# A hybrid two-block model on one core: every second lower part in the query and value sections made by GpSimd

## The chip, the cores and the metric

The kernel runs on one core of a Trainium2 chip. The metric is the device time of one execution in microseconds (us). A core has five engines with a queue of instructions each, and each queue runs in its own order: TensorE (PE; its weight loads are PEld), VectorE (DVE, here "the vector engine"), ScalarE (ACT), GpSimd (POOL) and SyncE (SP, which starts the weight transfers here). Engines wait for each other through semaphores. SBUF is the on-chip memory that all engines read; PSUM holds TensorE's results, in 8 banks of 128x512 f32.

## The reference

The input is 256 tokens of width 1024, in f32. Block one has two layers with two attentions each, block two has two layers of another kind; the change is in block two. Cut to what it touches:

```
h = rmsnorm(x, pre_mix_g);  proj = h @ w_in            # 1024 x D_IN
q, k, v = silu(conv4(concat(dn_q, dn_k, dn_v)))        # causal, 4 taps, each 1024 wide
q, k = l2norm(q) * 128 ** -0.5, l2norm(k)              # 8 heads of 128
o = gated_delta_rule(q, k, v, g, beta)                 # chunks of 64
y_a = (rmsnorm(o) * silu(dn_z)) @ w_up_dn
y_b = window_attention_with_sinks(sw_q, sw_k, sw_v) @ w_up_sw   # 16 query heads of 64
x = x + rmsnorm((sigmoid(gate_a) * y_a + sigmoid(gate_b) * y_b) @ w_o)
x = x + rmsnorm(relu(rmsnorm(x) @ w_ff1) ** 2 @ w_ff2)
```

## The kernel before

**Weights.** Every product with a weight matrix is made from two rounded numbers for each operand: the upper part (`hi`) is the value rounded to the fp32r type, the lower part (`lo`) is the rest. Three matmuls (lines 374 to 376) add hi·xh, lo·xh and hi·xl in PSUM. SP loads weights in units of 512 rows by 512 columns into one of 4 buffers `raw` (`load_unit`). A unit is two pieces: an even and an odd one, each 128 partitions by 1024 columns. ScalarE makes `hi` of a piece (`split_hi`, line 348), the vector engine makes `lo` by a subtraction of two SBUF tensors, `raw - hi` (`split_lo`, line 356). There are 4 buffers of `hi` and of `lo`; TensorE takes 12 matmuls for a piece (`multiply`) and then gives its buffers back. SP reloads a `raw` buffer when both lower parts of its unit are made.

**Order.** The plan (`plan_two`) is a list of steps written out by hand: a step ("piece", g), and after it small steps of other work. Every engine goes through the same list and does its share. At the step of piece g ScalarE makes the upper part of piece g+3 (`LEAD`), the vector engine the lower part of piece g+2 (`LO_LEAD`), and TensorE multiplies piece g.

**The stretch.** A section of 1024 columns is two jobs of 4 pieces. After the sections sq and ba (window attention's queries, keys, values and the gates' inputs) come dk, dq and dv, the inputs of the convolution, that is keys, queries and values. During dq and dv the small steps are:
- window attention, one head a step and three heads in the air: scores on TensorE (lines 1453 and 1454); the masked row maximum on the vector engine (`masked_max`: line 880 with a PSUM and an SBUF input, then 886 and 887 on 128x2 numbers in SBUF); exponentials on ScalarE (1716, 1719); turning on TensorE (1461), ScalarE's copy of the turned (1725), the weighted sum on TensorE (1469 to 1471). The row sums are finished on the vector engine by 1971 (an addition of two 128x2 tensors in SBUF) and 1973, the output by 1978;
- the convolution of the section before: two of four steps turn 2x128 channels (TensorE, line 398), and the vector engine puts the four taps on (1841, and 1843 six times, with one input in PSUM);
- for the keys: squares, their sums on TensorE (1441), copied by the vector engine (1889), and the reciprocal roots on GpSimd (893, 899).

On GpSimd stand, before the stretch, the rotations of the queries (lines 913 to 918), and after it the level masks of the delta rule (2097, 2106).

Of the kernel before, what the change touches and what calls it, by code (L numbers as in the profile page):

```python
# [17 lines left out]
F32 = mybir.dt.float32  # L18
F32R = mybir.dt.float32r
I32 = mybir.dt.int32  # L20
ALU = mybir.AluOpType
# [16 lines left out]
RAW = 4  # L38
RING = 4
LEAD = 3  # L40
LO_LEAD = 2
# [39 lines left out]
class Signals:  # L81
# [4 lines left out]
    def __init__(self, nc, ctx, prefix, tally=None):  # L86
        self.nc, self.ctx, self.prefix, self.tally = nc, ctx, prefix, tally
        self.sems, self.count, self.keys, self.stage = {}, {}, {}, 0

    def sem(self, name):  # L90
        if name not in self.sems:
            self.sems[name] = self.ctx.enter_context(self.nc.semaphore(f"{self.prefix}_{name}"))
        return self.sems[name]
# [167 lines left out]
class Core:  # L261


    def __init__(self, nc, ctx, ins, plans):
        self.nc, self.ctx, self.ins = nc, ctx, ins
        self.pieces = [piece for plan in plans for piece in plan.pieces]
        self.units = [(job, n, plan.layer) for plan in plans for job, n in plan.units]
        sb = lambda name, shape, dt=F32: ctx.enter_context(nc.sbuf_tensor(name, shape, dt))
        sem = lambda name: ctx.enter_context(nc.semaphore(name))
        self.x = sb("x_res", [P, TB, D])  # L270
        self.raw = [sb(f"raw{i}", [P, 4 * CH]) for i in range(RAW)]
        self.hi = [sb(f"hi{i}", [P, 2 * CH], F32R) for i in range(RING)]
        self.lo = [sb(f"lo{i}", [P, 2 * CH], F32R) for i in range(RING)]

        self.xh = [sb(f"xh{i}", [P, KB, S], F32R) for i in range(2)]
        self.xl = [sb(f"xl{i}", [P, KB, S], F32R) for i in range(2)]
        self.buf = [sb(f"buf{i}", [P, TB, D]) for i in range(9)]
        self.scratch = sb("scratch", [P, 5120])
        self.final_row = self.buf[3][:, 0, :]
        self.masks = sb("masks", [P, 3, S])  # L280
        self.square = sb("square", [P, 3 + LEVELS, P])
        self.rope1 = sb("rope1", [P, TB, 4, ROT // 2])
        self.rope2 = sb("rope2", [P, TB, 4, ROT // 2])
        self.ident, self.upper, self.ones = (self.square[:, i, :] for i in range(3))
        self.small = sb("small", [P, 850])
        self.small_used = 0
        self.bank = [ctx.enter_context(nc.psum_tensor(f"bank{i}", [P, CH], F32)) for i in range(8)]
        self.passed = sem("passed")
        self.last_read, self.turn_bank, self.hi_at, self.lo_at = {}, {}, 0, 0
        self.programs = {e: [] for e in ("tensor", "scalar", "vector", "gpsimd", "sync")}  # L290
        self.unit_loaded = [sem(f"unit_loaded{i}") for i in range(RAW)]
        self.hi_ready, self.lo_ready = sem("hi_ready"), sem("lo_ready")
        self.pieces_used = sem("pieces_used")

    def hold(self, s, bank, name, key=0):

        self.last_read[bank] = (s, name, key, s.stage)
# [26 lines left out]
    def load_unit(self, sp, u):  # L324

        job, n, layer = self.units[u]
        if u >= RAW:
            sp.wait_ge(self.lo_ready, 2 * (u - RAW) + 2)
        slot, k = u % RAW, job.unit
        r0 = (job.row + n * k) * P  # L330
        src = self.ins[job.weight][layer, r0:r0 + k * P, job.col:job.col + job.cols].rearrange("(k p) c -> p k c", p=P)
        dst = self.raw[slot][:, 0:k * job.cols].rearrange("p (k c) -> p k c", k=k)
        sp.dma_start(dst, src).then_inc(self.unit_loaded[slot], 16)
# [6 lines left out]
    def split_hi(self, act, upto):  # L340

        for g in range(self.hi_at, min(upto, len(self.pieces))):
# [5 lines left out]
            act.activation(self.hi[g % RING][:, 0:w], src, ACT.Copy).then_inc(self.hi_ready, 1)  # L348
            self.hi_at = g + 1

    def split_lo(self, dve, upto):

        for g in range(self.lo_at, min(upto, len(self.pieces))):
            src, w = self.piece_raw(g)
            dve.wait_ge(self.hi_ready, g + 1)
            dve.tensor_tensor(self.lo[g % RING][:, 0:w], src, self.hi[g % RING][:, 0:w].bitcast(F32),  # L356
                              ALU.subtract).then_inc(self.lo_ready, 1)
            self.lo_at = g + 1

    def multiply(self, pe, g, rows=(0, 1), blocks=(0, 1)):  # L360


        job, n = self.pieces[g]
        pe.wait_ge(self.lo_ready, g + 1)
        k, c, slot = job.unit // 2, job.cols, g % RING
        xh, xl = self.xh[job.xt], self.xl[job.xt]
        for kk in rows[:k]:
            row = job.xt_block + n * k + kk
            w = slice(kk * c, kk * c + c)
            for tb in blocks:  # L370
                out, t = self.bank[job.banks[tb]][:, 0:c], slice(tb * P, tb * P + P)
                first = job.start and n == 0 and kk == 0
                last = job.stop and n == job.pieces - 1 and kk == k - 1
                pe.matmul(out, xh[:, row, t], self.hi[slot][:, w], start=first, stop=False)  # L374
                pe.matmul(out, xh[:, row, t], self.lo[slot][:, w], start=False, stop=False)  # L375
                mm = pe.matmul(out, xl[:, row, t], self.hi[slot][:, w], start=False, stop=last)  # L376
        if rows[-1] >= k - 1 and blocks[-1] == TB - 1:
            mm.then_inc(self.pieces_used, 1)
        return mm
# [79 lines left out]
def rms(pool, s, waits, means, out, key):  # L459

    pool.wait_ge(*s.at("mean", waits[0]))
    pool.tensor_scalar(out, means[0], 1e-6, None, ALU.add).then_inc(*s.up("rms_first", key))  # L462
    pool.wait_ge(*s.at("rms_first", key))
    pool.wait_ge(*s.at("mean", waits[1]))
    pool.tensor_tensor(out, out, means[1], ALU.add).then_inc(*s.up("rms_sum", key))
    pool.wait_ge(*s.at("rms_sum", key))
    pool.tensor_tensor(out, out, s.minus_half[:, 0:out.shape[-1]], ALU.pow).then_inc(*s.up("rms", key))
# [774 lines left out]
def block_two(nc, core, s, plans, ins):  # L1242
# [815 lines left out]
    def _(pool):  # L2058
        for plan in plans:
            layer, base = plan.layer, plan.base  # L2060
            for what in plan.all_steps(s):
                kind, arg = what[0], what[1] if len(what) > 1 else None
                if kind == "rstd":
                    out = t.final_r if s.stage == DEPTH else t1.r[:, s.stage, :]
                    rms(pool, s, [(c, TB - 1) for c in range(2)], [t1.mean[:, s.stage, c, :] for c in range(2)], out, "final" if s.stage == DEPTH else "r")
# [14 lines left out]
                if kind == "post_x":  # L2080
                    tb = what[2]
                    i = 2 * layer + arg
# [117 lines left out]
```

## Time and profile before

| | |
|---|---|
| median of 3 runs | 1938.02 us (1937.54 to 1938.33) |
| the profiled execution | 1939.12 us, its span 1937.3 us |
| granted TensorE clock, mean | 0.987 |
| TensorE busy | 1853.9 us (96%) |
| vector engine busy | 1201.1 us (62%) |
| ScalarE busy | 921.5 us (48%) |
| GpSimd busy | 233.2 us (12%) |

The span is from the first to the last instruction of the profiled execution. Times inside the trace are us from its start; one "x15" is 15 instructions. "[0.42 <-ACT ...]" says that the engine was idle for 0.42 us before this instruction and which engine's instruction ended that. The granted clock is a share of 2.4 GHz. The names in "out<-in" are the program's own; a "buf", "small", "square" or "scratch" lies in SBUF, a "bank" in PSUM. Matmul rows overlap each other, since matmuls are pipelined.

### The profile page before, as it was taken

To read this page: it belongs to the slowest core of one execution; us is meant where nothing else is said; L and a number is where in the kernel's file an instruction comes from. 1 tells how busy PE (TensorE), PEld (TensorE's weight loads), DVE (VectorE), ACT (ScalarE), POOL (GpSimd) and SP (SyncE) were. 2 spreads that over 40 slices of the span, in tenths; PEclk is the share of its full clock that TensorE was granted. 3 is DMA by queue.
4 is the path that set the end of the run, shared out by engine and by line. 5 is a ranking of instruction groups with operands and counts; after the bars stand their busy time and mean duration, and the time that the engine had idled before them with its cause. 6 is when DMAs were issued, how large, how long until landed. Compare 5 with 4: busy or idle time off the path is not lost.

```text
span 1937.3 us, 25474 instructions
## 1 busy us (share of the span) xinstructions
PE 1853.9 (96%) x9623; PEld 1523.1 (79%) x9623; DVE 1201.1 (62%) x2323; ACT 921.5 (48%) x1624; POOL 233.2 (12%) x298
## 2 busy tenths in 40 slices
PE   5999999999999999999999989998999999999998
PEld 4877877887787788778888878887777888877887
DVE  4655667666566766676655665556586555665555
ACT  4354365434436645454433454445464333444443
POOL 0301100030030002102213000000201221200000
PEclk9999999999999999998999999999998999999999
DMA  6543534565343456232212445554433221354552
GB/s 242 165 146 114 169 127 164 168 197 170 109 152 131 139 177 206 99 110 81 72 66 87 153 152 196 174 181 164 135 109 95 66 80 66 113 189 155 174 188 95
DMA packets 136817, 270.15 MB, mean 139 GB/s; under 512 B 5500, under 2 KB 8312, under 8 KB 136696
## 3 DMA queue, kind: packets, MB, share of 16 engines
q1 hardware_dynamic: 134820, 265.75, 41.2%
q10 hardware_dynamic: 1876, 2.78, 0.4%
q8 instruction: 78, 1.28, 0.3%
q14 instruction: 43, 0.35, 0.1%
HBM read 267.46 MB, written 1.05 MB: 139 GB/s over the span
## 4 chain that ended last, share of the span: by engine, by line
PE 82%; DVE 9%; ACT 4%; issue 3%; POOL 1%; DMA 1%; SPq 0%; DVEq 0%; POOLq 0%; ACTq 0%
PE bank L374 21%; PE bank L376 21%; PE bank L375 21%; PE bank L398 3%; PE bank L1522 3%; PE bank L1536 2%; DVE buf L1843 2%; PE bank L1535 1%; DVE lo L356 1%; PE bank L1441 1%; DVE scratch L880 1%; PE bank L553 1%; PE bank L545 1%; ACT scratch L670 1%; PE bank L543 1%
## 5 line engine op out<-in xcount | busy, mean ns | idle before, releaser
L374 PE MATMUL bank<-hi,xh 128*128 128x512 f32 (+1 forms) x2016 | 821.5, 407 | 21.8 <-issue 12.0
L376 PE MATMUL bank<-hi,xl 128*128 128x512 f32 (+1 forms) x2016 | 791.4, 393 | 0.0
L375 PE MATMUL bank<-lo,xh 128*128 128x512 f32 (+1 forms) x2016 | 789.1, 391 | 0.0
L348 ACT ACTIVATE hi<-raw 128x1024 fp32r<-128x1024 f32 (+1 forms) x504 | 527.9, 1049 | 341.0 <-PE bank L376 338.8
L356 DVE TENSOR_TENSOR lo<-raw,hi 128x1024 fp32r<-128x1024 f32 (+1 forms) x504 | 610.7, 1225 | 90.1 <-ACT hi L348 89.7
L374 PEld LDWEIGHTS bank<-hi,xh 128*128 128x128 f32 x2016 | 383.6, 190 | 95.8 <-issue 19.3
L376 PEld LDWEIGHTS bank<-hi,xl 128*128 128x128 f32 x2016 | 382.0, 190 | 83.2
L375 PEld LDWEIGHTS bank<-lo,xh 128*128 128x128 f32 x2016 | 384.2, 191 | 68.9
L1740 ACT ACTIVATE scratch<-bank 128x512 f32<-128x512 f32 x48 | 28.7, 599 | 143.5 <-PE bank L1522 143.5
L398 PE MATMUL bank<-square,buf 128*128 128x128 f32 x584 | 87.9, 273 | 7.2 <-POOL buf L918 5.2
L398 PEld LDWEIGHTS bank<-square,buf 128*128 128x128 f32 x584 | 70.8, 140 | 23.8 <-issue 7.6
L880 DVE CUSTOM_DVE_ANT_0 scratch<-bank,masks 128x128 f32<-128x128 f32 (+1 forms) x128 | 40.6, 355 | 71.5 <-PE bank L545 50.2
L462 POOL TENSOR_SCALAR small<-small 128x1 f32<-128x1 f32 (+1 forms) x13 | 5.1, 390 | 605.1 <-ACT scratch L455 604.9
L1814 DVE TENSOR_TENSOR xl<-bank,xh 128x512 fp32r<-128x512 f32 x32 | 22.1, 692 | 78.1 <-ACT xh L1647 78.1
L1716 ACT ACTIVATE scratch<-scratch,small 128x128 f32<-128x128 f32 x64 | 28.6, 448 | 79.7 <-DVE small L887 79.7
L659 ACT ACTIVATE scratch<-scratch,small 128x128 f32<-128x128 f32 x64 | 28.7, 449 | 75.2 <-DVE small L887 75.2
L1843 DVE SCALAR_TENSOR_TENSOR buf<-bank,small,buf 128x255 f32<-128x255 f32 (+1 forms) x144 | 62.7, 477 | 2.5
L741 DVE TENSOR_SCALAR buf<-bank,small 128x512 f32<-128x512 f32 x48 | 33.8, 746 | 41.2 <-PE bank L376 41.2
L893 POOL TENSOR_SCALAR small<-small 128x4 f32<-128x4 f32 (+1 forms) x14 | 4.5, 324 | 451.3 <-ACT scratch L688 203.8
L2020 DVE TENSOR_TENSOR scratch<-scratch,bank 128x512 f32<-128x512 f32 (+1 forms) x48 | 28.7, 638 | 30.0 <-PE bank L1536 30.0
L1647 ACT ACTIVATE xh<-bank 128x512 fp32r<-128x512 f32 x32 | 19.2, 598 | 59.0 <-PE bank L398 59.0
L880 DVE CUSTOM_DVE_ANT_0 scratch<-bank,masks,small 128x128 f32<-128x128 f32 x64 | 24.1, 413 | 37.0 <-PE bank L1454 37.0
(269 smaller groups left out, 1981.9 us busy)
## 6 DMA issues: line engine op xcount, KB each, us to landing
raw<-in_w_in SPq DMA_DIRECT2D x136, 1024.0 KB, 5.0
raw<-in_w_ff SPq DMA_DIRECT2D x64, 1024.0 KB, 5.2
raw<-in_w_proj_a SPq DMA_DIRECT2D x8, 1024.0 KB, 5.0
raw<-in_w_proj_b SPq DMA_DIRECT2D x8, 1024.0 KB, 5.0
raw<-in_w_out SPq DMA_DIRECT2D x8, 1024.0 KB, 5.1
raw<-in_w_up_sw SPq DMA_DIRECT2D x8, 1024.0 KB, 5.0
raw<-in_w_up_dn SPq DMA_DIRECT2D x8, 1024.0 KB, 5.1
raw<-in_w_o SPq DMA_DIRECT2D x8, 1024.0 KB, 5.6
```

The source lines that it names most:

```text
L348: act.activation(self.hi[g % RING][:, 0:w], src, ACT.Copy).then_inc(self.hi_ready, 1)
L356: dve.tensor_tensor(self.lo[g % RING][:, 0:w], src, self.hi[g % RING][:, 0:w].bitcast(F32), ALU.subtract).then_inc(self.lo_ready, 1)
L374: pe.matmul(out, xh[:, row, t], self.hi[slot][:, w], start=first, stop=False)
L375: pe.matmul(out, xh[:, row, t], self.lo[slot][:, w], start=False, stop=False)
L376: mm = pe.matmul(out, xl[:, row, t], self.hi[slot][:, w], start=False, stop=last)
L398: mm = pe.transpose(bank[:, (j * TB + tb) * P:(j * TB + tb + 1) * P], src[:, tb, c:c + P], core.ident)
L659: ins = act.activation(prob[h % 2][:, 0, cols], masked[:, h % 2, cols], ACT.Exp, scale=SCALE, bias=t.negmax[:, h % 2, tb:tb + 1], accum_ou ...
L741: ins = dve.tensor_scalar(role[name][:, tb, cols], B[job.banks[tb]][:, :], t.r[:, s.stage, tb:tb + 1], None, ALU.mult)
L880: ins = dve.tensor_tensor_reduce(masked[:, cols], bank[:, cols], core.masks[:, which, keys], 1.0, NEG if sink is None else sink[0], ALU.ad ...
L1522: mm = pe.matmul(B[TURN][:, i * P:i * P + P], lm[l % 2][:, h, c, :], tr[g % 2][h][:, c, 0, :], start=True, stop=True)
L1536: mm = pe.matmul(o[:, P:2 * P], yy[:, h, c, :], tr[g % 2][h][:, c, 1, :], start=True, stop=True)
L1843: ins_ = dve.scalar_tensor_tensor(y, x, w, y, ALU.mult, ALU.add)
```

## The change

For the jobs dq0, dq1, dv0 and dv1 of either layer of block two the lower part of the odd pieces is made by GpSimd: 8 of the 16 pieces of a layer. GpSimd issues it at the step two pieces ahead, as the vector engine did, and before the other work of that step. It has its own semaphore, and TensorE and SP wait for the one that belongs to the piece. SP waits for both pieces of the unit one by one. The vector engine passes over these pieces.

```diff
@@ Core.load_unit
-            sp.wait_ge(self.lo_ready, 2 * (u - RAW) + 2)
+            for g in (2 * (u - RAW), 2 * (u - RAW) + 1):
+                sp.wait_ge(*self.lo_done(g))
@@ Core
+    def on_pool(self, g):
+
+        job, n = self.pieces[g]
+        return job.name in ("dq0", "dq1", "dv0", "dv1") and n % 2 == 1
+
+    def lo_done(self, g):
+
+        mine = self.on_pool(g)
+        return self.lo_pool if mine else self.lo_ready, sum(self.on_pool(i) == mine for i in range(g + 1))
+
+    def split_lo_pool(self, pool, g):
+
+        if g < len(self.pieces) and self.on_pool(g):
+            src, w = self.piece_raw(g)
+            pool.wait_ge(self.hi_ready, g + 1)
+            pool.tensor_tensor(self.lo[g % RING][:, 0:w], src, self.hi[g % RING][:, 0:w].bitcast(F32),
+                               ALU.subtract).then_inc(self.lo_pool, 1)
+
     def split_lo(self, dve, upto):
 
         for g in range(self.lo_at, min(upto, len(self.pieces))):
+            self.lo_at = g + 1
+            if self.on_pool(g):
+                continue
             src, w = self.piece_raw(g)
             dve.wait_ge(self.hi_ready, g + 1)
             dve.tensor_tensor(self.lo[g % RING][:, 0:w], src, self.hi[g % RING][:, 0:w].bitcast(F32),
                               ALU.subtract).then_inc(self.lo_ready, 1)
-            self.lo_at = g + 1
@@ Core.multiply
-        pe.wait_ge(self.lo_ready, g + 1)
+        pe.wait_ge(*self.lo_done(g))
@@ block_two, GpSimd's program
                 kind, arg = what[0], what[1] if len(what) > 1 else None
+                if kind == "piece":
+                    core.split_lo_pool(pool, base + arg + LO_LEAD)
```

## Rows read from the trace of the kernel before

**Rows 1.** Page, first part: busy us of each engine (share of the span).

```profile
PE 1853.9 (96%) x9623; PEld 1523.1 (79%) x9623; DVE 1201.1 (62%) x2323; ACT 921.5 (48%) x1624; POOL 233.2 (12%) x298
```

**Rows 2.** Windows: length, busy PE, PEld, DVE, ACT, POOL, granted clock, DMA share, GB/s.

```profile
793.39:876.71 83.32, 81.22 (x434) 63.41 (x434) 64.94 (x211) 45.65 (x116) 3.92 (x2) 0.96 0.28 90
1393.76:1478.77 85.01, 82.91 (x435) 65.54 (x434) 64.92 (x211) 45.64 (x116) 3.93 (x2) 0.94 0.27 88
```

**Rows 3.** Line 1469: its idle time, us and times, by releaser.

```profile
  ACT scratch L1725: 1.6, 4
```

**Rows 4.** Timeline of PE, 1396 to 1413.5: start, us, instruction, idle before.

```profile
1408.24 0.48 PE L374 MATMUL bank<-hi,xh 128*128 128x512 f32 x1
...
1412.52 0.41 PE L1469 MATMUL bank<-buf,scratch 128*128 128x64 f32 x2 [0.42 <-ACT scratch L1725]
```

**Rows 5.** Timeline of ACT, 1396 to 1448.

```profile
1396.14 1.04 ACT L348 ACTIVATE hi<-raw 128x1024 fp32r<-128x1024 f32 x1
...
1406.19 1.04 ACT L348 ACTIVATE hi<-raw 128x1024 fp32r<-128x1024 f32 x1
...
1411.91 0.47 ACT L1725 ACTIVATE scratch<-bank 128x384 f32<-128x384 f32 x1
...
1415.71 1.06 ACT L348 ACTIVATE hi<-raw 128x1024 fp32r<-128x1024 f32 x1
...
1426.09 1.05 ACT L348 ACTIVATE hi<-raw 128x1024 fp32r<-128x1024 f32 x1
...
1447.82 1.04 ACT L348 ACTIVATE hi<-raw 128x1024 fp32r<-128x1024 f32 x1
```

**Rows 6.** Timeline of DVE, 1396 to 1431.

```profile
1398.61 0.23 DVE L886 TENSOR_SCALAR small<-small 128x2 f32<-128x2 f32 x1
...
1398.82 0.15 DVE L1971 TENSOR_TENSOR small<-small 128x2 f32<-128x2 f32 x1
...
1402.58 1.21 DVE L356 TENSOR_TENSOR lo<-raw,hi 128x1024 fp32r<-128x1024 f32 x1
1403.71 0.34 DVE L880 CUSTOM_DVE_ANT_0 scratch<-bank,masks,small 128x128 f32<-128x128 f32 x1
...
1408.67 1.21 DVE L356 TENSOR_TENSOR lo<-raw,hi 128x1024 fp32r<-128x1024 f32 x1
1409.80 0.34 DVE L880 CUSTOM_DVE_ANT_0 scratch<-bank,masks,small 128x128 f32<-128x128 f32 x1
...
1418.72 0.15 DVE L1971 TENSOR_TENSOR small<-small 128x2 f32<-128x2 f32 x1
...
1422.48 1.21 DVE L356 TENSOR_TENSOR lo<-raw,hi 128x1024 fp32r<-128x1024 f32 x1
...
1428.57 1.21 DVE L356 TENSOR_TENSOR lo<-raw,hi 128x1024 fp32r<-128x1024 f32 x1
```

**Rows 7.** Groups by line, DVE, 1393.76 to 1478.77: busy us, mean ns, idle before.

```profile
L356 DVE TENSOR_TENSOR lo<-raw,hi 128x1024 fp32r<-128x1024 f32 x15 | 18.1, 1210 | 0.0
```

**Rows 8.** Lines 2106 and 918: duration in ns, shortest, median, longest; starts; forms.

```profile
L2106 POOL TENSOR_TENSOR scratch<-buf,square x24: 1269/1292/2302, 895.6 to 1625.5; 128x512 f32<-128x512 f32 x24
L918 POOL TENSOR_TENSOR buf<-scratch x24: 323/741/1292, 54.1 to 1380.3; 128x256 f32<-128x256 f32 x20, 128x64 f32<-128x64 f32 x4
```

**Rows 9.** Timeline of POOL, 1395 to 1530, the key norms.

```profile
1467.78 1.00 POOL L893 TENSOR_SCALAR small<-small 128x16 f32<-128x16 f32 x1 [86.75 <-DVE small L1889]
1468.87 2.93 POOL L899 TENSOR_TENSOR small<-small 128x16 f32<-128x16 f32 x1
```

**Rows 10.** Waits of the SP queue, 1380 to 1490: us, times, longest.

```profile
SPq L333 <- DVE lo L356: 99.7, 9, 16.0
```

**Rows 11.** Timeline of POOL and DVE near 1498; line 2012, durations in ns.

```profile
1497.64 2.25 POOL L2106 TENSOR_TENSOR scratch<-buf,square 128x512 f32<-128x512 f32 x1
...
1498.69 1.74 DVE L2012 TENSOR_TENSOR buf<-square,buf 128x512 f32<-128x512 f32 x1
...
L2012 DVE TENSOR_TENSOR buf<-square,buf x4: 679/1213/1744, 896.6 to 1584.5; 128x512 f32<-128x512 f32 x4
```

More of the change, by code:

```diff
@@ L293, in __init__ @@
         self.pieces_used = sem("pieces_used")
+        self.lo_pool = sem("lo_pool")
     def hold(self, s, bank, name, key=0):
```

## The prediction

> **What bounds the kernel now.** The page's busy row comes first: TensorE is busy for 96% of the span, the vector engine for 62%, GpSimd for 12% [rows 1]. The change touches 16 vector instructions of more than two thousand, so the share says little, and the stretch has to be looked at by itself. In the windows of the query and value sections (from the first product of dq0 to the first of the last piece of dv1, once in each layer) TensorE is busy for 81.22 of 83.32 us and 82.91 of 85.01 us, the vector engine for 64.9 us of either [rows 2]. So TensorE sets the end here too, and what the vector engine is spared counts only where TensorE waits for a chain that runs through it. The list of what TensorE's weighted sums of the window attention (line 1469) waited for names one releaser, the copy of the turned probabilities on ScalarE (line 1725), 4 times in the whole trace and 1.6 us together [rows 3].
>
> The timelines tell what stands behind the longest of these. Of this chain, step by step: scores on TensorE, row maximum on the vector engine (lines 880, 886, 887), exponentials on ScalarE, then ScalarE's copy, then TensorE's sum. At 1412.52 TensorE begins line 1469 after 0.42 us of waiting [rows 4]; the copy began at 1411.91 [rows 5]; it stood behind the exponentials of a maximum begun at 1409.80, and that one behind a lower part from 1408.67, 1.21 us long, itself behind convolution taps and, before these, a maximum at 1403.71 that followed the lower part of 1402.58 [rows 6]. That last one is of an odd piece: it is one that goes.
>
> **The parts of the change.** *Removed from the vector engine:* 8 lower parts in a layer, 16 in all, of 1.21 us each in this stretch [rows 7], 19.4 us of its time. Nearly all of it lies beside TensorE's work. Where it lies on a chain, the gain is bounded by the waits of rows 3: 1.6 us for all four, two in a layer: the one at 1412.52, and one that ScalarE's own work ends. Four steps after the first the same chain recurs and comes out even with TensorE, without a wait that the view lists.
>
> *Added on GpSimd:* 16 subtractions of 128x1024. The trace has none of this size. From both sides: the level masks of 128x512 take 1292 ns (median; 1269 the shortest), the rotation's sum of 128x256 takes 741 [rows 8]. The difference, 551 ns for 256 columns, put on twice gives 1292 + 1102 = 2.39 us. Twice 1292 would be 2.58; the longest GpSimd instruction of 512 columns, 2302 [rows 8], doubled would be 4.6 and is the upper end; the vector engine's own 1.21 is the lower end. I take 2.4, since the two nearest sizes point to it.
>
> *Is it in time?* The upper part is ready by 1397.18 (begun 1396.14, 1.04 long [rows 5]), and TensorE takes up that piece at 1408.24 [rows 4]: 11.1 us for an operation of 2.4. Even 4.6 is covered. GpSimd has nothing else in the stretch but the two instructions of the key norms (1467.78 and 1468.87, 3.93 us busy [rows 2, 9]). The last odd piece stands behind them in GpSimd's order and is then ready near 1474.2, TensorE takes it up at 1478.77, the end of the window of rows 2: 4.6 us left. The first of the two was itself held: 1.00 us, while the lower part of that last piece ran on the vector engine; this goes, and is off the path. If the cover were gone, a piece would be late by what the operation exceeds these 11.1 us by.
>
> *The weight queue:* SP waits for both lower parts before it reloads a buffer, 99.7 us of waiting in 9 times for line 356 in this stretch [rows 10]. It will be released by GpSimd at about 1399.6 in place of 1403.8, and similarly for six more; the last is later by 5.5 us (1474.2 for 1468.7). ScalarE's upper parts don't wait for weights here, so I price both at 0; the added wait instruction of SP costs nothing, as it only stands before transfers that wait anyway. On TensorE one wait is replaced by another.
>
> *The new collision.* An instruction of either engine can be lengthened by the other's. GpSimd's mask at 1497.64 takes 2.25 us against the 1.29 of rows 8, and the vector engine's product of two SBUF tensors (line 2012) at 1498.69 takes 1.74 against 0.68 at the shortest [rows 11]: the later waits until the other's instruction is over. The Trainium skill (SBUF — State Buffer, Who interferes with whom) says that a vector instruction with two SBUF inputs and a GpSimd instruction that reads SBUF exclude each other for the whole instruction; by that rule too, the trace agrees, with 1.06 us on that product. So a GpSimd subtraction of 2.39 us can hold back line 1971 (two small SBUF inputs) and the even lower parts of line 356. Taking the second layer, with the ready times of the upper parts from [rows 5] and the vector engine's from [rows 6]:
>
> First case. GpSimd works 1397.2 to 1399.6. Line 1971 wants to begin at 1398.82 and is held to 1399.6: +0.8. The taps behind it end 0.8 later (1403.5), but the lower part of 1402.58 is gone, so the maximum begins at 1403.45 in place of 1403.71 (−0.26). The next upper part (1406.19) moves with it to 1405.93, and GpSimd works 1407.0 to 1409.4. The vector engine is through with its taps at 1408.67 − 0.26 = 1408.4, wants the even lower part and is held to 1409.4; the maximum of 1409.80 begins at 1410.55: **+0.75**, and this is on the chain to TensorE's wait at 1412.52.
>
> Second case, everything 0.75 later. Upper part of 1415.71: ready at 1417.5, GpSimd to 1419.9; line 1971 (1418.72 + 0.75 = 1419.47) held by 0.45. The taps end 0.45 later, the lower part that followed them at 1422.5 is gone, so the next maximum comes 0.55 earlier than in step; it moves the upper part of 1426.09 to an end at 1427.3; GpSimd to 1429.75; the even lower part (1428.57 + 0.75 − 0.55 = 1428.8) is held by 1.0; net 1.0 − 0.55 = **+0.45** on a chain that had nothing to spare.
>
> In the value section the GpSimd subtractions fall beside taps, which read one operand from PSUM, and I find no further cost. The sum of a layer is 0.75 + 0.45 = 1.2 us, of both layers 2.4 us. The profiled execution would go from 1939.12 (span 1937.3 and 1.8 around it) to 1941.5. It stands 1.1 us above the median of 1938.02, and the comparison is of medians: 1938.0 + 2.4 = **1940.4 us**.
>
> **The rivals.** *B, the chain gets shorter:* GpSimd's operation is shorter than 2.4 us or falls beside the vector engine's PSUM work; the freed 1.21 us ends the four waits of rows 3, −1.6 us: 1936.4. For it: the even lower part is held only because it comes about 1 us too early in either case, and the freed 1.21 us is more than that. Against it: GpSimd is started by the upper part of the same step in which the even lower part stands, so that the two meet by their order.
>
> *C, the small instructions are held too (slower):* lines 886 and 887 work on one SBUF operand [rows 6], and the maximum can't be told to ScalarE before 887. No row shows one of them beside a GpSimd instruction, so nothing in the trace excludes it. Then it is line 886 at 1398.61 that is held to 1399.6, 0.2 more than in the first case, and 0.4 more in the second; and a third place comes in, the step of the upper part of 1447.82 [rows 5]: GpSimd works from 1448.9 to 1451.3, over the whole of that maximum's small instructions, an estimated 0.4 of it on TensorE. A layer costs 1.2 + 0.6 + 0.4 = 2.2, both 4.4: 1942.4. It decides as soon as the exclusion holds for one-input SBUF instructions. The Trainium skill (SBUF — State Buffer, Who interferes with whom) says that a vector tensor_scalar in a 2-port mode excludes GpSimd as well; no run here shows it yet.
>
> *D, GpSimd's operation is long:* at 3.5 us each of the four holds of a layer grows by 1.1, 4.4 us in a layer: about 1949.
>
> *E, the clock:* the same stretch takes 83.32 us at a granted clock of 0.96 and 85.01 at 0.94 [rows 2], 1.7 us for the same work. If the shift of a few tenths moves a stretch at 1.2 GHz, each layer may change by 1.7 either way: with B, 1936.4 − 3.4 = 1933.0, with A 1943.8.
>
> *F, the vector engine was the bound after all:* −19.4, 1918.6; against it stand the 2.1 us that TensorE is idle in each window.
>
> **How the numbers follow.** A (the forecast) 0.50, B 0.17, C 0.22, D 0.04, E 0.06 (half each way), F 0.01. A measurement of this kernel tells some 0.2% (3.9 us) from no change: faster means below 1934.1, slower above 1941.9. B and most of A lie within. Slower: most of C (0.19), D, half of E and a tail of A (0.04), 0.30. Faster: half of E, F and little more, 0.05. Same: 0.65. The range goes from B less a little to C and a mild D: 1936.0 to 1943.5.
>
> **What would show it.** The GpSimd rows of the new subtraction should have a shortest near 2.4 us; line 1971 a few instances near 0.6 to 1.0 us in place of 0.15; line 356, two or so in a layer of some 2.2 us; TensorE's wait before line 1469 near 1 us where it was 0.42. Line 886 tells A from C: 0.23 in all instances, or some near 1 us. I am wrong if the wait before line 1469 is gone (B), if TensorE waits for GpSimd’s lower part (too late), or if the two windows change by over 3 us with none of these rows.

## The result: 0.28% slower, and what the profile shows after the change

| | before | after |
|---|---|---|
| median of the 14 runs of each kernel | 1937.93 us (1936.03 to 1942.0) | 1943.77 us (1939.85 to 1944.84) |
| ratio to before, 95% interval | | 1.0028 (1.0020 to 1.0037) |
| the profiled execution | 1939.12 us, span 1937.3 | 1942.28 us, span 1940.5 |

The ratio makes 5.4 us (3.9 to 7.2), more than the 0.2% (3.9 us) that a measurement of this kernel was said to tell from no change; only the lower end of the interval touches it. The forecast was +2.4 us, and no measurable change as the likeliest case.

The numbers of lines rise by 22 behind the new code: 356 is now 379, 880 and 886 are 902 and 908, 1469 is 1491, 1725 is 1747, 1971 is 1993, 913 and 918 are 935 and 940. GpSimd's subtraction is line 368. The first row of the page answers to [rows 1]:

```profile
PE 1853.2 (96%) x9623; PEld 1522.8 (78%) x9623; DVE 1193.5 (62%) x2307; ACT 921.6 (47%) x1624; POOL 271.6 (14%) x314
```

16 instructions have gone from the vector engine, but it is busy for only 7.6 us less, where 16 times 1.21 is 19.4 us. Of the other 11.8 us, 5.7 have come back in line 908 and 3.8 in line 379, as held instructions. The last 2.3 us are in the way of counting: the page counts once where two rows overlap, and the durations themselves add up to 9.5 us less (1279.8 before, 1270.3 after). The view by line, duration in ns (shortest, median, longest), shows on which lines; for line 379 the window is the second layer's, 1385 to 1484:

```profile
L368 POOL TENSOR_TENSOR lo<-raw,hi x16: 2359/2382/3400, 790.0 to 1475.8; 128x1024 fp32r<-128x1024 f32 x16
L908 DVE TENSOR_SCALAR small<-small x32: 228/228/1575, 796.6 to 1484.9; 128x2 f32<-128x2 f32 x32
L1993 DVE TENSOR_TENSOR small<-small x32: 143/149/153, 801.4 to 1487.2; 128x2 f32<-128x2 f32 x32
L379 DVE TENSOR_TENSOR lo<-raw,hi x9: 1203/1217/2109, 1388.7 to 1483.0; 128x1024 fp32r<-128x1024 f32 x9
```

Line 908, two numbers per partition with one SBUF input, takes 0.23 us as a rule and up to 1.58. The timelines of GpSimd and of the vector engine (start, us, instruction, idle before), second layer, show why; the vector engine's answer to [rows 6]:

```profile
1402.55 2.38 POOL L368 TENSOR_TENSOR lo<-raw,hi 128x1024 fp32r<-128x1024 f32 x1 [6.63 <-ACT hi L350]
1412.30 2.38 POOL L368 TENSOR_TENSOR lo<-raw,hi 128x1024 fp32r<-128x1024 f32 x1 [7.37 <-ACT hi L350]
...
1454.36 3.40 POOL L368 TENSOR_TENSOR lo<-raw,hi 128x1024 fp32r<-128x1024 f32 x1 [5.68 <-ACT hi L350]
```

```profile
1403.90 1.05 DVE L908 TENSOR_SCALAR small<-small 128x2 f32<-128x2 f32 x1
...
1413.65 2.11 DVE L379 TENSOR_TENSOR lo<-raw,hi 128x1024 fp32r<-128x1024 f32 x1
1415.68 0.34 DVE L902 CUSTOM_DVE_ANT_0 scratch<-bank,masks,small 128x128 f32<-128x128 f32 x1
...
1454.29 1.22 DVE L379 TENSOR_TENSOR lo<-raw,hi 128x1024 fp32r<-128x1024 f32 x1
1455.42 0.35 DVE L902 CUSTOM_DVE_ANT_0 scratch<-bank,masks,small 128x128 f32<-128x128 f32 x1
...
1456.21 1.57 DVE L908 TENSOR_SCALAR small<-small 128x2 f32<-128x2 f32 x1
```

The reader is to add start and duration. GpSimd works from 1402.55 to 1404.93, and line 908, begun at 1403.90, ends at 1404.95. GpSimd works from 1412.30 to 1414.68; the lower part begun at 1413.65 needs 1.21 us and ends at 1415.76. The last three rows are both directions in a chain: the vector engine's lower part (to 1455.51) holds GpSimd's, which then takes 3.40 us in place of 2.38 and ends at 1457.76, and that one holds line 908 up to 1457.78. In between, the maximum of line 902, which reads PSUM, takes its 0.35 us and isn't held. Each layer has five holds of line 908 or of the lower part on the chain of the window attention: 0.82, 0.91, 0.67, 0.88 and 1.35 us.

What TensorE's weighted sums waited for (against [rows 3]), and its timeline where they did, second layer (against [rows 4]):

```profile
  ACT scratch L1747: 4.4, 8
```

```profile
1418.40 0.41 PE L1491 MATMUL bank<-buf,scratch 128*128 128x64 f32 x2 [1.01 <-ACT scratch L1747]
...
1438.73 0.41 PE L1491 MATMUL bank<-buf,scratch 128*128 128x64 f32 x2 [0.42 <-ACT scratch L1747]
1449.12 0.41 PE L1491 MATMUL bank<-buf,scratch 128*128 128x64 f32 x2 [0.40 <-ACT scratch L1747]
1459.48 0.41 PE L1491 MATMUL bank<-buf,scratch 128*128 128x64 f32 x2 [0.41 <-ACT scratch L1747]
```

The first was 0.42 us, the third was there before (0.40 at 1442.81) and is the one that the prediction put down to ScalarE's own work; the second and the fourth are new. That is 0.59 + 0.42 + 0.41 = 1.42 us in a layer. The windows from the scores of head 0 to those of head 13 say the same (columns as in [rows 2]); here the granted clock is 1.00, 2.4 GHz, from end to end in both kernels. Before, both layers:

```profile
792.54:856.27 63.73, 62.90 (x335) 48.38 (x335) 53.08 (x174) 41.70 (x103) 0.00 (x0) 1.00 0.32 105
1392.91:1456.64 63.73, 62.90 (x336) 48.38 (x335) 53.06 (x174) 41.69 (x103) 0.00 (x0) 1.00 0.32 105
```

After:

```profile
794.69:859.85 65.16, 62.95 (x335) 48.39 (x335) 51.48 (x168) 41.31 (x103) 15.28 (x6) 1.00 0.33 111
1398.20:1463.34 65.14, 62.91 (x336) 48.38 (x335) 51.51 (x168) 41.30 (x103) 15.28 (x6) 1.00 0.33 111
```

TensorE's busy time is the same and the stretch is 1.42 us longer. Since it varies by hundredths from one execution to the next, this **stretch** is the measure of the experiments. Both layers together are +2.84 us; the rest of the 5.4 lies elsewhere, and what is said of the missing term below is about that.

SP's list of waits for weights, 1385 to 1495, shows GpSimd as the releaser where [rows 10] had the vector engine; TensorE waits for no lower part of GpSimd's anywhere:

```profile
SPq L330 <- POOL lo L368: 88.3, 8, 20.0
SPq L330 <- DVE lo L379: 8.7, 1, 8.7
```

### The profile page after: what moved, and what is told of

The parts are those of the page before. It is cut to its first block, busy times and chain, and to the rows that moved or that the text cites. A ratio compares the mean times of both kernels' runs of the same rounds, so it can differ in the third digit from the quotient of the medians.

```text
span 1940.5 us, 25722 instructions
## 1 busy us (share of the span) xinstructions
PE 1853.2 (96%) x9623; PEld 1522.8 (78%) x9623; DVE 1193.5 (62%) x2307; ACT 921.6 (47%) x1624; POOL 271.6 (14%) x314
## 3 DMA queue, kind: packets, MB, share of 16 engines
HBM read 267.46 MB, written 1.05 MB: 138 GB/s over the span
## 4 chain that ended last, share of the span: by engine, by line
PE 81%; DVE 9%; ACT 4%; issue 3%; POOL 1%; DMA 1%; SPq 0%; DVEq 0%; POOLq 0%; ACTq 0%
PE bank L396 21%; PE bank L398 21%; PE bank L397 21%; PE bank L420 3%; PE bank L1544 3%; DVE buf L1865 2%; PE bank L1558 2%; PE bank L1557 1%; DVE lo L379 1%; PE bank L1463 1%; DVE scratch L902 1%; PE bank L575 1%; PE bank L567 1%; ACT scratch L692 1%; PE bank L565 1%
## 5 line engine op out<-in xcount | busy, mean ns | idle before, releaser
L379 DVE TENSOR_TENSOR lo<-raw,hi 128x1024 fp32r<-128x1024 f32 (+1 forms) x488 | 595.1, 1233 | 81.7 <-ACT hi L350 81.2
L368 POOL TENSOR_TENSOR lo<-raw,hi 128x1024 fp32r<-128x1024 f32 x16 | 40.1, 2504 | 107.6 <-ACT hi L350 107.6
```

The costliest lines, as they stand in the source:

```text
L368: pool.tensor_tensor(self.lo[g % RING][:, 0:w], src, self.hi[g % RING][:, 0:w].bitcast(F32), ALU.subtract).then_inc(self.lo_pool, 1)
```

## The experiments

They were measured in three groups, each on one chip beside 21 runs of the kernel before (medians 1937.84, 1937.74 and 1937.80 us). "Waits" is the list ahead of the weighted sum: us and times in both layers. "Clock" is the mean granted clock over all timed executions of the kernel; the 63 of before have 0.9880. The edits shift the numbers of lines by up to 5 more: line 908 is 909 in e4 and 911 in e7, line 1993 is 1998 in e4, line 379 is 380 in e7, line 368 is 372 in e7.

| kernel | stretch, layers 1 / 2 | waits | median us (runs) | ratio [95%] | clock |
|---|---|---|---|---|---|
| before, again | 63.75 / 63.75 | | 1937.97 (11) | 0.9999 [0.9990, 1.0008] | 0.9881 |
| after, again | 65.17 / 65.17 | | 1945.14 (5) | 1.0039 [1.0026, 1.0051] | 0.9846 |
| e1, subtraction left out | 62.77 / 62.77 | none | 1938.52 (11) | 1.0006 [0.9997, 1.0015] | 0.9856 |
| e2, made by both | 68.92 / 68.89 | 8.7, 8 | 1951.65 (5) | 1.0074 [1.0061, 1.0086] | 0.9836 |
| e3, put beside taps | 62.77 / 62.77 | none | 1938.12 (11) | 1.0004 [0.9995, 1.0013] | 0.9863 |
| e4, one column at a time | 66.56 / 65.05 | 4.2, 6 | 1944.09 (4) | 1.0034 [1.0021, 1.0048] | 0.9860 |
| e5, lower parts freed | 63.42 / 63.41 | 0.9, 2 | 1938.06 (11) | 1.0001 [0.9993, 1.0010] | 0.9871 |
| e6, small ones freed | 63.43 / 63.46 | 1.1, 4 | 1938.64 (11) | 1.0008 [0.9999, 1.0017] | 0.9868 |
| e7, GpSimd only writes | 63.73 / 63.73 | 1.7, 4 | 1939.39 (1) | | 0.987 |
| e10, one layer | 65.13 / 63.73 | 3.0, 6 | 1940.11 (11) | 1.0015 [1.0006, 1.0024] | 0.9867 |
| e8, turning later | 63.76 / 63.75 | | 1931.11 (5) | 0.9967 [0.9954, 0.9979] | 0.9896 |
| e9, e3 and e8 | 62.77 / 62.77 | | 1930.61 (5) | 0.9965 [0.9952, 0.9977] | 0.9880 |

**The changed kernel and the one before, once more.** No edit.

> The changed kernel once more, beside the others. Theory X (exclusion): a GpSimd subtraction of 2.38 us holds back five vector instructions in a layer (line 908 by 0.82, 0.67 and 1.35 us, the even lower part by 0.91 and 0.88), TensorE's waits before line 1491 grow from 1.6 to 4.4 us over both layers, and what is left of +5.5 us is the clock: +2.8 from the waits in every execution, granted clock about 0.985 where the kernel before has 0.987 or more. Rival Y (nothing but clock phase): the ratio would move by 0.1% or more between sets of runs, with the same waits. Expected: 1.0025 to 1.0032 times the kernel before.

> The kernel before under another name, as a measure of what a comparison shows of nothing. Ratio 0.9995 to 1.0005, stretch 63.73. If it comes out at 1.0005 or above, the small excess of the runs with a shorter stretch (1.0001 to 1.0008) is of the measurement; if it is 1.000, that excess is of these kernels, and the clock is the candidate.

The stretches repeat to 0.02 us. The changed kernel's second median is 1.4 us above its first, and the second ratio, 1.0039, lies above the 1.0025 to 1.0032 expected; the two intervals overlap, so the stretch is certain to hundredths and the total is not known to better than about 1 us.

**The relief alone, and the exclusion alone.** e1:

```diff
 def lo_done(self, g):
-        return self.lo_pool if mine else self.lo_ready, ...
+        return (self.hi_ready, g + 1) if mine else (self.lo_ready, ...)
 ... GpSimd's program
-                    core.split_lo_pool(pool, base + arg + LO_LEAD)
+                    pass
```

> The odd lower parts of the four jobs are made by no engine (TensorE multiplies what the buffer held before; part of the computation is left out): the vector engine is spared all the same, and GpSimd does nothing in their place. X: no instruction is held; the wait of 0.42 us before line 1491 goes in each layer, and perhaps the second: 1936.4 to 1937.5, ratio 0.999 to 1.000. Rival Z (something else of the change costs, as the added semaphore waits of SP or TensorE, or a shifted order that the clock punishes): it stays near 1943.

e2, in which the vector engine makes all lower parts as before, and GpSimd makes the odd ones too, into memory that nobody reads, while TensorE and SP wait for both:

```diff
-            pool.tensor_tensor(self.lo[g % RING][:, 0:w], src, ...
+            pool.tensor_tensor(self.scratch[:, 3072:4096], src, ...
 ... split_lo
-            if self.on_pool(g):
-                continue
```

> The vector engine makes all lower parts, as before, and GpSimd makes the same 16 subtractions besides, into unused scratch columns; TensorE and SP wait for both. So the exclusion without the relief. X: the holds of the changed kernel come on top of a vector engine with 1.21 us more in every second step: more than the changed kernel, 1944 to 1949, TensorE's waits before its line 1491 above 4.4 us. If the relief was worth nothing, the same as the changed kernel (1943.5). Rival Z: at or below 1940.

The relief is worth 0.96 us in a layer (63.73 to 62.77), after which TensorE is busy for the whole stretch; in the total it doesn't show (1.0006, 0.9997 to 1.0015), though 1.9 us would be 0.9990; the missing term below takes this up. The exclusion by itself costs 5.2 us in a layer: 3.5 of waits (8.7 against 1.6, both layers) and 1.7 for 3.4 us at 1.2 GHz that lie inside the stretch. In the changed kernel the two meet: 0.96 us is gained and 2.4 us (62.77 to 65.16) paid for it. Both totals came out above what was expected: 1938.5 for 1936.4 to 1937.5 in e1, 1951.7 for 1944 to 1949 in e2. In e1 TensorE's waits before line 1491 are all gone, the third one of a layer too (0.40 before). So that one hung on the vector engine as well, not on ScalarE's own work alone. Theory F, that the vector engine is the bound, falls with e1: 19.4 us taken away bring 1.9 us of stretch.

**Is it where the subtraction falls?** In e3 GpSimd waits, before an odd piece, until the small instructions of that step's head are done, so that it runs beside the taps. The work is the same.

```diff
+                    if base + arg + LO_LEAD < len(core.pieces) and core.on_pool(base + arg + LO_LEAD):
+                        head = arg + LO_LEAD - plan.end["dk1"] - 4
+                        if head >= 0:
+                            pool.wait_ge(*at("s_inverse", head))
                     core.split_lo_pool(pool, base + arg + LO_LEAD)
```

> GpSimd starts the subtraction for local piece L (23 to 35) only when the vector engine has finished the small instructions of head L-23, that is, mostly beside the taps, which read PSUM. Same work on the same engines as in the changed kernel, only later. X: line 908 held at most twice in a layer and by under 0.6 us, no even lower part held; 1936.5 to 1938.5. Rival Y or Z: GpSimd's work itself or the clock costs, then it stays at 1942 to 1944. If waiting makes a lower part late, TensorE's line 397 shows a wait and the time exceeds 1940.

In e3, the durations by line (ns; line 379 in the second layer's window):

```profile
L368 POOL TENSOR_TENSOR lo<-raw,hi x16: 2356/2384/2413, 790.3 to 1470.5; 128x1024 fp32r<-128x1024 f32 x16
L908 DVE TENSOR_SCALAR small<-small x32: 228/228/231, 796.9 to 1479.1; 128x2 f32<-128x2 f32 x32
L379 DVE TENSOR_TENSOR lo<-raw,hi x11: 1204/1216/1225, 1387.6 to 1482.4; 128x1024 fp32r<-128x1024 f32 x11
```

None is held on either side, and the stretch is that of e1 to the hundredth. GpSimd's 2.38 us beside taps cost the stretch nothing; so the whole price of the change in the stretch is where the subtraction falls. The total is that of before (1.0004), again without the 1.9 us.

**Which hold matters?** e5 keeps the wait of e3 for heads 2 and 6 alone (the even lower parts go free), e6 for heads 0, 4 and 10 (the small instructions go free):

```diff
-                        if head >= 0:
+                        if head in (2, 6):       # e5;  e6: (0, 4, 10)
```

> The changed kernel, only the two GpSimd subtractions of a layer that held back an even lower part wait for the small instructions of the head (heads 2 and 6), so these holds (0.91 and 0.88 us) go; the three of line 908 (0.82, 0.67, 1.35) stay. The holds stand in series on one chain that has some 1 us of slack, so taking away either kind should take most of the price: stretch 63.2 to 63.8 (changed kernel 65.16, without any hold 62.77), total 1938 to 1940. If the even lower parts are what costs alone: 62.8 to 63.0. If line 908 is what costs alone: 65.

> The other way round: the three GpSimd subtractions that held line 908 wait (heads 0, 4 and 10), the two that hold even lower parts don't. Line 908 is held nowhere, line 379 twice in a layer by 0.9 us or more. My first and second case in the prediction were made of this kind plus line 1971; if the kinds are in series: stretch 63.2 to 63.8, total 1938 to 1940. If line 908 alone costs: 62.8 to 63.0. If the even lower parts alone: about 65.

Either one brings the stretch from 65.16 to 63.4, so 1.7 of the 2.4 us are gone each time, and the two savings are not to be added. In e5's second layer line 908 still takes 1.05, 0.64, 0.89 and 1.57 us, in e6's the lower parts of line 379 still take 2.08 and 2.10 us. What is left of TensorE's waits, in e5 and then in e6, second layer:

```profile
1456.28 0.41 PE L1491 MATMUL bank<-buf,scratch 128*128 128x64 f32 x2 [0.43 <-ACT scratch L1747]
```

```profile
1412.92 0.41 PE L1491 MATMUL bank<-buf,scratch 128*128 128x64 f32 x2 [0.16 <-ACT scratch L1747]
...
1443.20 0.41 PE L1491 MATMUL bank<-buf,scratch 128*128 128x64 f32 x2 [0.39 <-ACT scratch L1747]
```

So the changed kernel's four waits have different grounds. At the first two (1.01 and 0.42) a hold of line 908 and one of a lower part follow each other on one chain that had about 1 us to spare (the 0.96 of e1), and with either kind gone the rest is nearly covered: no wait in e5, 0.16 in e6. The fourth wait (0.41) belongs to line 908 alone; e5 keeps it in full (0.43), and in e6 it is gone. The third (0.40), which the kernel before has too, stays in e6 (0.39) and is gone in e5. That the first hold is swallowed and only the next is paid for fits the first two places; no run takes the holds away one at a time.

**Which instructions are held?** e4 makes the two 128x2 instructions of lines 886 and 887 as two of 128x1 each:

```diff
-        dve.tensor_scalar(sink[1], top[:, :], sink[0], -SCALE, ALU.subtract, ALU.mult)
+        for i in range(2):
+            dve.tensor_scalar(sink[1][:, i:i + 1], top[:, i:i + 1], sink[0], -SCALE, ALU.subtract, ALU.mult)
+        for i in range(2):
+            ins = dve.tensor_scalar(negmax[:, i:i + 1], top[:, i:i + 1], -SCALE, None, ALU.mult)
```

> The changed kernel, with lines 908 and 909 (128x2) each cut into two instructions of 128x1 in the window attention. If a one-operand vector instruction is held back by GpSimd only where it can run its operand through two ports (the Trainium skill, VectorE: DVE Perf Modes, Mode 2x_2P, wants the outermost dimension that isn't one to be even, which one column has not), none of them is held: longest under 0.3 us; line 1993 behind them is held in their place, which doesn't delay the maximum. Stretch from the scores of head 0 to those of head 13: about 64.4 us where the changed kernel has 65.16 and the one before 63.73; total 1941 to 1943. If the exclusion is for any one-operand SBUF instruction: held as before, up to 1.5 us, and slower than the changed kernel by the added instructions, 1943.5 to 1946.

In e4, GpSimd's timeline and then the vector engine's:

```profile
1401.55 2.38 POOL L368 TENSOR_TENSOR lo<-raw,hi 128x1024 fp32r<-128x1024 f32 x1 [6.76 <-ACT hi L350]
```

```profile
1402.74 0.34 DVE L909 TENSOR_SCALAR small<-small 128x1 f32<-128x1 f32 x2
1403.00 0.20 DVE L911 TENSOR_SCALAR small<-small 128x1 f32<-128x1 f32 x2
1403.12 0.83 DVE L1998 TENSOR_TENSOR small<-small 128x2 f32<-128x2 f32 x1
```

While GpSimd works, up to 1403.93, the four instructions of one column pass, and the addition of two SBUF tensors behind them (1971 before) stays until 1403.95. In the whole trace none of the 128 instructions of one column is held (longest 216 ns). The stretch hardly cares, 65.05 for 65.16, and not the 64.4 expected. The fourth wait of TensorE is gone, as line 908 alone had made it, but the first is 1.34 us in place of 1.01: what held a small instruction now holds the next one, or the even lower part behind it. The first layer's stretch, 66.56, has 3.4 us at 1.2 GHz in it (less half of that it is 64.86); the second has none. The Trainium skill says both things: a tensor_scalar whose operands all lie in SBUF takes the second port where their outermost dimension that isn't one is even, or odd and the same on both sides (VectorE: DVE Perf Modes, Mode 2×_2P), and an instruction in such a mode and one of GpSimd shut each other out (SBUF — State Buffer, Who interferes with whom). This case's runs agree in what is held: 128x2 up to 1.58 us, 128x1 at most 0.22. The ports themselves no trace shows.

e7 asks whether GpSimd excludes by reading. It is e2 with a memset in place of the subtraction:

```diff
-            pool.tensor_tensor(self.scratch[:, 3072:4096], src, ...
+            pool.memset(self.scratch[:, 3072:4608], 0.0).then_inc(self.lo_pool, 1)
```

> The vector engine makes all lower parts as before; GpSimd, at the 16 places, only fills 1536 scratch columns with zeros, which reads nothing from SBUF. If the exclusion of two-input instructions is by the read side (the Trainium skill, SBUF: State Buffer, Who interferes with whom), no instruction of line 381 is held in this stretch, while 128x2 instructions (line 912), which may use two write ports, still may be: stretch near 63.7 to 64.7, one run 1937 to 1941. If reading or writing makes no difference: lower parts held as in the run with both, stretch over 65.

The memset takes 1.38 us, not 2.4, so the single number of the stretch (63.73, as before) proves less than hoped. What counts are the places where the two overlap; GpSimd's row first, then the vector engine's:

```profile
1390.97 1.38 POOL L372 MEMSET scratch<- 128x1536 f32 x1 [7.19 <-ACT hi L352]
```

```profile
1390.94 1.23 DVE L380 TENSOR_TENSOR lo<-raw,hi 128x1024 fp32r<-128x1024 f32 x1 [3.50 <-ACT hi L352]
```

Both run side by side at full length, as at 790.3 and at 1451.7. Against a subtraction begun so, GpSimd's row is 3.40 us long. So an instruction of GpSimd that only writes leaves the vector engine's of two SBUF inputs alone. No small instruction met a memset for more than 0.01 us, so for 128x2 with one input this stays open.

**One layer of two.** Only the first layer of block two has the change:

```diff
-        return job.name in ("dq0", "dq1", "dv0", "dv1") and n % 2 == 1
+        return self.units[g // 2][2] == 0 and job.name in ("dq0", "dq1", "dv0", "dv1") and n % 2 == 1
```

> The change in the first of the two layers of block two alone. The waits of the changed kernel add 1.43 us in a layer, its total is 5.5 to 7 us up. If the price is per layer: stretch 65.16 in the first, 63.73 in the second, total +2.7 to +3.5, 1940.5 to 1941.5, ratio 1.0014 to 1.0018. If the part above the waits comes from anything that doesn't scale with the layers (phase of the clock), the total lies anywhere between 1938 and 1943.

The stretch is 65.13 and 63.73: +1.40 us. The total is +0.15% (0.06 to 0.24), 2.9 us (1.2 to 4.7) with a median 2.3 us up. So the price of the stretch goes layer by layer, and the total, about half of the 5.4 us, agrees with it.

**A version that beats both.** In the kernel before, TensorE's longest waits near the change are for GpSimd's rotation of the queries. TensorE, then the vector engine, then GpSimd, before:

```profile
1381.17 0.63 PE L398 MATMUL bank<-square,buf 128*128 128x128 f32 x4 [2.58 <-POOL buf L918]
```

```profile
1366.89 3.49 DVE L356 TENSOR_TENSOR lo<-raw,hi 128x1024 fp32r<-128x1024 f32 x3
1371.08 1.22 DVE L356 TENSOR_TENSOR lo<-raw,hi 128x1024 fp32r<-128x1024 f32 x1 [0.70 <-ACT hi L348]
1376.48 2.61 DVE L356 TENSOR_TENSOR lo<-raw,hi 128x1024 fp32r<-128x1024 f32 x2
```

```profile
1367.06 3.43 POOL L913 TENSOR_TENSOR scratch<-buf,rope 128x32 f32<-128x32 f32 x1 [22.68 <-DVE buf L1929]
1370.45 0.25 POOL L914 TENSOR_TENSOR scratch<-buf,rope 128x32 f32<-128x32 f32 x1
...
1376.73 1.28 POOL L913 TENSOR_TENSOR scratch<-buf,rope 128x128 f32<-128x128 f32 x1
1377.98 1.43 POOL L914 TENSOR_TENSOR scratch<-buf,rope 128x128 f32<-128x128 f32 x1
```

It is the same exclusion the other way round: a GpSimd instruction of 0.25 us takes 3.43, behind three lower parts in a row. Behind the two of 1376.48 it is otherwise. The second of them, by itself:

```profile
1377.75 1.35 DVE L356 TENSOR_TENSOR lo<-raw,hi 128x1024 fp32r<-128x1024 f32 x1
```

GpSimd's line 913 of 1376.73 ends at 1378.01, and the second lower part takes 1.35 us in place of 1.22. Here GpSimd got its turn between the two, and line 914 was held by the second. Both layers show the same, and why it is so at one place and not at the other is open. e8 is the kernel before with the turning of the first queries one piece later; e9 is e3 with the same:

```diff
-                         [("turn", "sk", 0)]] + turns("sq", 0, 3) + [turns("sq", 3)[0] + work[0]])
+                         [("turn", "sk", 0)], [], turns("sq", 0)[0] + turns("sq", 1)[0], turns("sq", 2)[0],
+                         turns("sq", 3)[0] + work[0]])
```

> The kernel before, with one line of the plan changed: in the key section the first turn of the attention's queries (which needs GpSimd's rotation) comes one piece later, together with the second. In the kernel before, TensorE waits 2.58 us in each layer for that rotation (start 1381.17), and its GpSimd instructions are themselves held back by the vector engine's lower parts (line 913: 3.43 us for 0.25 of work, then 1.28 for 0.46, line 914 1.43 for 0.46, line 918 1.28 for 0.32, by the timeline of the kernel before), the same exclusion as in the changed kernel, the other way round; piece 373 and its lower part are ready at 1372.3. Theory X: the wait goes, and the 3.41 us at half clock that follow it at 1382 may go too: 2 x 2.58 = 5.2 us, with the clock up to 8.6: 1929 to 1933, ratio 0.996 to 0.997. Rival: something else in that place is as late (ScalarE's copies, banks), under 1 us gained.

> The same plan line on top of the kernel in which GpSimd's subtractions run beside the taps. X: the stretch from head 0 to head 13 is 62.77 (before 63.73) and the wait for the rotation is gone: 1.9 us below the run with the plan line alone, 1927 to 1932. Rival (the gain in the stretch is given back, as in the run with GpSimd beside the taps, which came out at 1.0004): equal to the run with the plan line alone.

TensorE in e8, where it turns the first queries, and the windows from 1355 to 1400 of before and of e8 (two fences):

```profile
1379.12 1.06 PE L398 MATMUL bank<-square,buf 128*128 128x128 f32 x8 [0.75 <-POOL buf L918]
```

```profile
1355.00:1400.00 45.00, 42.42 (x196) 34.12 (x196) 21.68 (x47) 22.12 (x36) 13.22 (x20) 0.96 0.47 156
```

```profile
1355.00:1400.00 45.00, 44.25 (x216) 35.44 (x215) 27.08 (x59) 22.65 (x41) 14.11 (x20) 1.00 0.46 148
```

The two waits fall from 5.2 to 1.5 us, and the clock, 1.2 GHz for 3.4 us right behind the 2.58 us wait of before, stays at 2.4 in e8 there. The kernel gets 6.4 us faster (0.9967, 0.9954 to 0.9979), 3.7 of them waits. e9 was expected 1.9 us below e8 if the shorter stretch counted; it is 0.5 below (0.9965), which can't be told from nothing, as the rival had it.

## Where the prediction was right and where it missed: point by point

**The number.** The forecast was 1940.4 us in a range of 1936.0 to 1943.5. The ratio put on its starting point of 1938.0 gives 1943.4, just inside; the median of 1943.77 itself is just outside. It is slower, as forecast, but by more than twice the 2.4 us, and that it still falls at the edge of the range is luck: 2.84 us come from the stretch, in good part by another instruction than forecast, and some 2.6 from a term that the sum put at nothing.

**Right: GpSimd's duration.** Worked out from two sizes as 2.39 us, measured 2.38. Case D had no ground.

**Right: in time, and the weights.** TensorE waits for no lower part of GpSimd's, and the weight queue's shift shows no cost: e3, which gives its buffers back later still, has the stretch of e1.

**Right in its place, a little too large: the first case.** +0.75 us on the chain, measured +0.59 on the wait (0.42 to 1.01, the "near 1 us" that was to be looked for).

**Right in size: the second case.** +0.45, measured +0.42.

**Wrong: "lines 1971 and the even lower parts are held" (A), with line 886 left free.** Line 908, the old 886, is held and the old 1971 never is, since it comes behind it. The text had line 886 at 0.23 in all instances for A and some near 1 us for C, and it was C. With this comes C's third place, the step of head 10, forecast at 0.4 us and measured at 0.41: the term that A lacked; e4 and e6, in which line 908 isn't held there, have no wait there. C's own addition for the first two cases, 0.6 us in a layer, was not there: the waits grew by 0.59 and 0.42, close to A's 0.75 and 0.45. That GpSimd's end sets the delay whichever instruction is held fits e4, where line 1998 goes free at the same moment. So a layer costs 1.42 us: A had 1.2, C 2.2. The row that would have told this could not be read from the trace before, where no small instruction met one of GpSimd. C was given 0.22 as an open case; the error was to give A, by the same silence, more than twice as much.

**Wrong: the second wait of a layer.** The prediction put the one of 0.40 us down to ScalarE's own work; e1 ends it by freeing the vector engine. So the relief was worth both waits of a layer.

**Wrong: the sum.** The stretches add 2.84 us where the sum had 2.4, and 2.84 would still have been no measurable change. **The missing term**, some 2.6 us of the 5.4, goes with a lower granted clock. 10 of the 14 timed executions of the changed kernel had a mean of 0.985; of the 21 of before beside e8, 16 had 0.988. A line through the means of before, after, both repeats, e1, e3, e5, e6, e8, e9 and e10 (e2 and e4 left out, as 1.2 GHz lies inside their stretches), with the TensorE time that each kernel's trace adds or takes (both stretches, and e8's 3.7) as one term and the clock as the other, gives 1.1 us for each us of that and 1.3 us for each 0.001 of clock; all eleven lie within 0.35 us of it. For the change that is 2.84 us of waits and 0.0024 of clock, 3.1 + 3.1 = 6.2 us by the line, where the means are 6.0 apart (1943.5, and 1937.5 of the 63 runs of before). It is an account, not a cause: clock and time are read from the same executions. (A profiled execution alone misled here: 0.988 after and 0.987 before, and 3.2 us between their spans.)

Why the clock is lower is open, but two explanations fall. It is not TensorE's waiting: e1 and e3 wait less than before and have 0.9856 and 0.9863. It is not GpSimd's work: e1 has none of it. All kernels with the odd lower parts off the vector engine are lower than their counterpart without, e10 (one layer) by 0.0013 and e1 (both) by 0.0024, e9 than e8 by 0.0016. But freeing the vector engine can't be all of it: in e2 it makes every lower part, and the clock is 0.9836; the 6.8 us at 1.2 GHz in its two stretches are worth 0.0017 of that, and 0.985 is still below before. One rival was not tested: before and e8, which have the higher clock, are the kernels without the changed waits of SP and TensorE, and the kernels with the lower one all have them. No run has these waits alone. In the rows the spells at 1.2 GHz lie outside the stretch (but for e2 and e4), and the profiled executions differ in how many there are. Case E had a shift of the clock of the right size (1.7 us a layer, against some 1.5), but at 0.06, even on both sides, and as a rival to A where it came on top of it. That was the costliest error: with the line's 3.1 us for it, A itself ends at 1938.0 + 2.4 + 3.1 = 1943.5.

**B, the gain.** The relief is real, 0.96 us in a layer (e1), about the two waits of [rows 3], as B had it. It can't be had with the subtraction in that place; in e3 it can, and there the total doesn't show it, beside a lower clock: at one and the same mean clock of 0.987, e3's four executions have a median of 1936.6 and the ten of before one of 1938.5. TensorE sets the end, and of the vector engine's 19.4 us only these 1.9 were on its path.

## What to carry to other kernels

Work moved to GpSimd is priced by what the vector engine wants at that moment: put a subtraction that reads SBUF beside vector work that reads PSUM (e3: nothing held, no cost in the stretch), and not beside small SBUF instructions or products of two SBUF tensors on a chain to TensorE (1.4 us in a layer for 19.4 us of relief in two). Look for the exclusion in a profile by the longest against the shortest duration of one line, on both engines, before anything is moved: here it pointed to 6.4 us. Beside each time stands its mean granted clock, since a change can come with a shift of it that is worth as much as its own waits. Where two holds stand in series on one chain with some slack, taking away either kind can bring back most of the price (1.7 of 2.4 us here, e5 and e6), so their savings are not to be added.

## What was not expected of the hardware

- An instruction of 128x2 numbers with one SBUF input, 0.23 us by itself, stays for as long as GpSimd's subtraction runs: up to 1.58 us. With 128x1 it passes (e4: 128 instructions, longest 0.22).
- The holding goes on from engine to engine: lower part on the vector engine, 1.22 us, GpSimd's held to 3.40, and line 908 held by that one to 1.57.
- GpSimd can be kept waiting through several vector instructions that stand back to back: 0.25 us became 3.43 behind three of them. Between the two of 1376.48 it did get its turn.
- A memset of 128x1536 on GpSimd (1.38 us) and a lower part on the vector engine (1.23) overlap without either getting longer.
